# A two-layer hybrid decoder step on one core: reordering the linear attention's masks, convolution taps and norm steps

## The reference

```python
xn = rmsnorm(x); z = xn @ w_in + b_in
o_a = rmsnorm(gla(q, k, v, log_a, state)) * silu(r)      # gated linear attention, chunks of 64
o_b = gelu(u) * spatial(layernorm(gelu(v)))              # gMLP
o_c = silu(layernorm(causal_depthwise_conv31(c_a * sigmoid(c_g))))
o_d = sink_attention(q, k, v)                            # window of 128, learned sinks
x = x + (sum_b sigmoid(xn @ w_gate_b) * (o_b @ w_branch_b)) @ w_out
x = x + swiglu(rmsnorm(x))
```

## Time and profile before

| | |
|---|---|
| median of three runs | 1078.9 us (1078.13 to 1079.26) |
| the profiled execution | 1078.94 us |
| its span, first to last instruction | 1077.1 us |
| outside the span | 1.84 us |
| PE busy in the span | 1070.7 us |
| DVE, ACT, POOL busy | 739.7, 585.9, 454.4 us |

### The profile page before, as it was taken

One profiled execution on the slowest core, in us unless ns is written; L12 is line 12 of the kernel. 1 busy time (PEld: TensorE's weight loads), 2 busy tenths in 40 slices (PEclk: granted clock), 3 DMA queues, 4 the chain that ended last, 5 costly groups with the idle time before them and its releaser, 6 DMA issues.

```text
span 1077.1 us, 20930 instructions
## 1 busy us (share of the span) xinstructions
PE 1070.7 (99%) x8755; PEld 1054.6 (98%) x8755; DVE 739.7 (69%) x1020; ACT 585.9 (54%) x895; POOL 454.4 (42%) x248
## 2 busy tenths in 40 slices
PE   9999999999999999999999999999999999999999
PEld 9999989999999999999999999999999999999998
DVE  6699999565875555555548799894577765555542
ACT  7664654778455444444446656567774564444431
POOL 2777845773742111101177768657737321111000
PEclk9999999999999999999999999999999999999999
DMA  9754553444555765555545555445454655555552
GB/s 294 257 172 162 171 158 103 141 152 155 176 172 185 217 200 185 170 174 162 175 152 158 159 168 181 159 121 155 157 154 140 232 164 170 160 174 161 175 172 83
DMA packets 65053, 182.53 MB, mean 169 GB/s; under 512 B 17056, under 2 KB 21792, under 8 KB 64288
## 3 DMA queue, kind: packets, MB, share of 16 engines
q1 hardware_dynamic: 63952, 177.12, 52.6%
q10 hardware_dynamic: 1008, 4.08, 1.0%
HBM read 174.90 MB, written 7.27 MB: 169 GB/s over the span
## 4 chain that ended last, share of the span: by engine, by line
PE 89%; DVE 10%; ACT 1%; issue 0%; DVEq 0%; ACTq 0%
PE ps L457 29%; PE ps L462 28%; PE ps L458 28%; DVE ps L1380 2%; DVE work L1354 1%; PE ps L780 1%; DVE zg L1454 1%; DVE work L1429 1%; PE ps L657 0%; DVE qz L1507 0%; PE ps L477 0%; DVE hist_p L1340 0%; DVE zg L1446 0%; DVE zg L1447 0%; DVE work L1445 0%
## 5 line engine op out<-in xcount | busy, mean ns | idle before, releaser
L457 PE MATMUL ps<-x_hi,w_hi 128*128 128x288 f32 x1952 | 583.2, 299 | 0.0
L458 PE MATMUL ps<-x_lo,w_hi 128*128 128x288 f32 x1952 | 575.8, 295 | 0.0
L462 PE MATMUL ps<-x_hi,w_lo 128*128 128x288 f32 x1952 | 574.0, 294 | 0.0
L930 ACT ACTIVATE w_hi<-raw 128x1024 fp32r<-128x1024 f32 x314 | 326.1, 1052 | 143.2 <-PE ps L462 130.0
L1779 POOL TENSOR_TENSOR w_lo<-raw,w_hi 128x1024 fp32r<-128x1024 f32 x129 | 335.2, 2612 | 162.3 <-ACT w_hi L930 161.1
L457 PEld LDWEIGHTS ps<-x_hi,w_hi 128*128 128x128 f32 x1952 | 365.8, 187 | 6.4 <-issue 4.7
L462 PEld LDWEIGHTS ps<-x_hi,w_lo 128*128 128x128 f32 x1952 | 367.4, 188 | 0.0
L458 PEld LDWEIGHTS ps<-x_lo,w_hi 128*128 128x128 f32 x1952 | 366.5, 188 | 0.4
L1296 DVE TENSOR_TENSOR w_lo<-raw,w_hi 128x1024 fp32r<-128x1024 f32 x185 | 230.1, 1245 | 119.6 <-ACT w_hi L930 119.6
L1803 POOL TENSOR_TENSOR work<-work,rs 128x288 f32<-128x288 f32 x44 | 35.9, 815 | 238.2 <-ACT work L1257 238.2
L462 PE MATMUL ps<-h_hi,w_lo 128*128 128x288 f32 x352 | 104.4, 296 | 0.0
(11 more groups left out here) (249 smaller groups left out, 1076.7 us busy)
## 6 DMA issues: line engine op xcount, KB each, us to landing
raw<-in_w_up SPq DMA_DIRECT2D x88, 512.0 KB, 4.1
raw<-in_w_z SPq DMA_DIRECT2D x66, 512.0 KB, 3.7
raw<-in_w_gate SPq DMA_DIRECT2D x64, 512.0 KB, 3.6
raw<-in_w_branch SPq DMA_DIRECT2D x32, 512.0 KB, 3.6
raw<-in_w_down SPq DMA_DIRECT2D x32, 512.0 KB, 3.5
raw<-in_w_out SPq DMA_DIRECT2D x16, 512.0 KB, 3.6
raw<-in_w_down SPq DMA_DIRECT2D x16, 384.0 KB, 3.3
kv<-in_state ACTq DMA_DIRECT2D x2, 1024.0 KB, 5.0
```

The source lines that it names most:

```text
L457: pe.matmul(out, wh, rh, start=start, stop=False)
L458: pe.matmul(out, wh, rl, start=False, stop=False)
L462: return pe.matmul(out, w_lo[:, slot, u * UNIT:(u + 1) * UNIT], rh, start=False, stop=stop)
L930: act.activation(w_hi[:, slot, :], raw[:, slot, :], ACT.Copy).then_inc(hi_done, 1)
```

## The change

- In ACT's generator `conv0` moves behind `k_copied`, to place 41.
- In DVE's order for layer 0, the convolution steps ahead of segment 11 (the masks) go from 14 to 4 and those ahead of segment 12 from 3 to 10. In layer 1 those ahead of segment 12 go from 3 to 0. What is not run by then is run later, in segment 17 at the latest.
- Scores are kept with their sign turned: the score step multiplies by `-HD ** -0.5` and subtracts the mask, the reduction is a minimum, and the exponential is taken with `scale=-1.0`. `softmax_in` then has two instructions in place of three.
- The differences for `to_last` are two instructions for both key tiles in place of four.
- `conv1`, `cv_mean`, `cv_sq`, `gla_sums`, `gla_rstd`, `gla_spread`, `r_silu`, `c_silu`, `a_parts` and `smp_update0` go two places later. `gm_mean`, `gates0` and all that follows keep their places.

```diff
-    chunk1=42, chunk2=43, chunk3=44, gla_spread=53, n1_sums=0, n1_rstd=0, n1_sums0=3, n1_rstd0=3, c_gate0=12,
+    chunk1=42, chunk2=43, chunk3=44, gla_spread=55, n1_sums=0, n1_rstd=0, n1_sums0=3, n1_rstd0=3, c_gate0=12,
-    exp0=20, exp1=31, prompt_pv=36, prompt_od=37, smp_scores=27, conv0=40,
-    conv1=48, exp_s=30, probs_s_turned=34, probs_s_copied=35, smp_pv=36, smp_od=37, decay_in=24, decay_y=16, decay_log=17,
+    exp0=20, exp1=31, prompt_pv=36, prompt_od=37, smp_scores=27, conv0=41,
+    conv1=50, exp_s=30, probs_s_turned=34, probs_s_copied=35, smp_pv=36, smp_od=37, decay_in=24, decay_y=16, decay_log=17,
-    gla_o=37, cv_mean=49, cv_sq=50, smp_update0=57, smp_update1=58, gla_sums=52, gla_rstd=52, cv_var=39, r_silu=54,
-    c_silu=56, a_parts=51, gates0=60, gm_mean=60, gm_sq=61, gm_var=63, gv_done=64, gv_turned=65, gv_copied=68,
+    gla_o=37, cv_mean=51, cv_sq=52, smp_update0=59, gla_sums=54, gla_rstd=54, cv_var=39, r_silu=56,
+    c_silu=58, a_parts=53, gates0=60, gm_mean=60, gm_sq=61, gm_var=63, gv_done=64, gv_turned=65, gv_copied=68,
-CONV_RUNS = (8, 1, 0, 0, 0, 2, 0, 0, 0, 3, 6, 14, 3, 2, 3, 4, 4, 5, 2, 4, 9, 10, 8, 9, 10, 7, 3,
-             8, 2, 0, 4, 5, 2, 0, 0, 0, 3, 3, 7, 3, 2, 3, 4, 4, 0, 6, 7, 4, 13, 0, 11, 13, 7, 3)
+CONV_RUNS = (8, 1, 0, 0, 0, 2, 0, 0, 0, 3, 6, 4, 10, 2, 3, 4, 4, 5, 2, 4, 9, 10, 8, 9, 10, 7, 3,
+             8, 2, 0, 4, 5, 2, 0, 0, 0, 3, 3, 7, 0, 2, 3, 4, 4, 0, 6, 7, 4, 13, 0, 11, 13, 7, 3)
...
                 act.wait_ge(E("v_turned"), l1)
-                yield from at("conv0")
-                conv_out(l, 0)
                 yield from at("k_copied")
                 act.wait_ge(E("k_turned"), l1)
+                yield from at("conv0")
+                conv_out(l, 0)
...
-                link(dve.tensor_tensor(small[:, 0, cols], small[:, 0, cols], p("sink", 0, 18)[:, cols], ALU.max), l)
-                dve.tensor_scalar(small[:, 1, cols], small[:, 0, cols], -1.0, None, ALU.mult)
-                dve.tensor_tensor(small[:, 2, cols], p("sink", 0, 18)[:, cols], small[:, 0, cols], ALU.subtract)\
-                    .then_inc(E(event), 1)
+                sink = p("sink", 0, 18)[:, cols]
+                link(dve.scalar_tensor_tensor(out=small[:, 1, cols], in0=sink, scalar=-1.0, in1=small[:, 0, cols],
+                                              op0=ALU.mult, op1=ALU.min), l)
+                dve.tensor_tensor(small[:, 2, cols], sink, small[:, 1, cols], ALU.add).then_inc(E(event), 1)
...
-                for k in range(2):
-                    v, w = to_last[:, k, 0:SEQ].rearrange("p (n i) -> p n i", i=64), decays[:, k, 0:SEQ].rearrange("p (n i) -> p n i", i=64)
-                    dve.tensor_tensor(v, w[:, :, 63:64].to_broadcast([P, NSEG, 64]), w, ALU.subtract)
-                    v, w = to_last[:, k, SEQ:T].rearrange("p (n i) -> p n i", i=DEC_T), decays[:, k, SEQ:T].rearrange("p (n i) -> p n i", i=DEC_T)
-                    ins = dve.tensor_tensor(v, w[:, :, DEC_T - 1:DEC_T].to_broadcast([P, DEC_B, DEC_T]), w, ALU.subtract)
+                v, w = (a[:, :, 0:SEQ].rearrange("p k (n i) -> p k n i", i=64) for a in (to_last, decays))
+                dve.tensor_tensor(v, w[:, :, :, 63:64].to_broadcast([P, 2, NSEG, 64]), w, ALU.subtract)
+                v, w = (a[:, :, SEQ:T].rearrange("p k (n i) -> p k n i", i=DEC_T) for a in (to_last, decays))
+                ins = dve.tensor_tensor(v, w[:, :, :, DEC_T - 1:DEC_T].to_broadcast([P, 2, DEC_B, DEC_T]), w, ALU.subtract)
-                                         scalar=HD ** -0.5, in1=bcast(c("band", P, P), 8), op0=ALU.mult, op1=ALU.add)\
+                                         scalar=-HD ** -0.5, in1=bcast(c("band", P, P), 8), op0=ALU.mult, op1=ALU.subtract)\
-                link(dve.tensor_reduce(small[:, 0, 0:8], prob0, AX.X, ALU.max), l)
+                link(dve.tensor_reduce(small[:, 0, 0:8], prob0, AX.X, ALU.min), l)
...
```

## The result

| | before | after |
|---|---|---|
| median of 7 runs each | 1079.11 us (1078.13 to 1079.26) | 1081.92 us (1081.3 to 1083.03) |
| ratio, 95% interval | | 1.003 [1.0021, 1.0039] |
| profiled execution | 1078.94 us | 1082.99 us |

The change made the kernel slower by 2.8 us, 0.3%. The forecast was 1082.4 us.

What follows compares the result with a forecast made beforehand. PE was taken as the bound, so only its waits and the slow clock behind them count: -4.4 + 0 + 7.9 = +3.5 us on 1078.94 us gives 1082.4 us, range 1079.0 to 1087.5 us.

Steps and rivals of the forecast that it cites:

- What bounds the kernel: PE is busy 1070.7 of 1077.1 us, so the change acts only through PE's waits and the slow clock behind them.
- Part 1: `conv0` behind `k_copied`, masks ahead of taps: layer 0's 2.6 us pause at `chunks` and 1.8 us slow clock go, -4.4 us.
- The state step: First state copy, layer 0 at `chunk1`: 1.1 us late by the rows, but taken as no wait; bounds 0 and 1.1 + 1.8 us.
- Part 2: Lighter softmax input and `to_last`: DVE gains 0 to about 3 us a layer, none of it PE's; worth 0.
- Part 3: Norms and state update two tiles later, `gm_mean` staying: 2.6 us wait there per layer plus 1.35 us slow clock, +7.9 us.
- X: Start of L745, PE's state update `smp_update0`, from which times up to `gm_mean` are counted.
- The price of the clock: Slow clock behind each new pause at `gm_mean`: bounds 0 and 1.8 us, three quarters taken, 1.35 us.
- Pause without slow clock: Rival: both waits at `gm_mean` come but PE's clock stays, 1079.7 us; chance 0.2, with one short fall included.
- Port held: Rival: POOL's block falls on DVE's difference L1317 as before, lengthening the waits at `gm_mean`, 1087.5 us; chance 0.1.
- Pause moved to `chunk1`: Rival: the pause at `chunks` only moves to `chunk1`, up to 2.9 of 4.4 us come back, 1085.3 us; chance 0.1.
- Faster, as `gm_mean` hardly waits: Rival: DVE has the sum ready within about a tile; without any wait 1074.5 us; chance 0.08.

Runs made afterwards that it cites:

- norms_one_later: Changed kernel with norm steps and state update one place later than before instead of two, and `gates0` at 59: 1074.62 us, ratio 0.9958.
- conv0_behind: Kernel before with one edit, `conv0` behind `k_copied` at 41 in ACT's order: 1077.8 us, ratio 0.9991.
- norms_back: Changed kernel with norm steps and state update, `conv1` and `gla_spread` back at their old places: 1077.39 us, ratio 0.9985.
- old_softmax: Changed kernel with the old score sign, three instructions in `softmax_in` and four for the differences: 1081.4 us.
- pause_filled: Changed kernel with 18 matmuls whose result nothing reads put ahead of the wait at `gm_mean`: 1080.26 us, ratio 1.0013.
- norms_one_gates60: Changed kernel with norm steps and state update one place later than before instead of two, `gates0` left at 60: 1077.67 us, ratio 0.9989.
- norms_later_alone: Kernel before with only the norm steps and state update moved two places later; `conv0`, taps and softmax as they were: 1086.41 us, ratio 1.0069.

## Why the prediction was right, step by step

**What bounds the kernel.** Right. The places where PE waited, and the clock behind them, account for the difference that matters most: norms_one_later has no wait at a mixer step, and the span of the changed kernel's profiled execution is 1081.2 - 1072.9 = 8.3 us longer; two pauses of 2.5 us and two falls of the clock at 1.6 us (both below) make 8.2. Between the medians it is 1081.92 - 1074.62 = 7.3 us.

**Part 1, -4.4 us.** Right in place and size, as a term of this sum. Between the kernel before and norms_one_later lie 1078.92 - 1074.62 = 4.3 us, and PE took up `chunk1` at 170.68 us before and at 166.56 after. The masks were named as the next cause, and conv0_behind shows them. The state step was named too, but that is less sure: in conv0_behind it was in time in layer 0, with PE held 1.5 us by the masks ahead of it, and late in layer 1, where the prediction saw nothing at stake. Nor is 4.4 us what parts 1 and 2 are worth alone. norms_back gained 1.5 us (1078.93 to 1077.39). Without its pause PE comes to `cv_mean` of layer 0 at 192.44 us in place of 196.23, and DVE's sum ends at 193.72 in place of 195.38, so what had been in time is late. Part 3 takes that wait away again; the prediction has no term for either, and they don't show in the total. In the changed kernel the state copy ended at 165.80 us, against 165.5 forecast, with L1532 at 0.69 us, against an estimate of 0.7.

**Part 2, nothing.** Right (old_softmax). At the place shown, the hold of 2.3 us went over to the next instruction.

**Part 3, +7.9 us.** The mechanism was right, and the size about right: 7.3 us from norms_one_later to the changed kernel, 7.5 us for part 3 on the kernel before. On parts 1 and 2 alone it is 4.5 us (1077.39 to 1081.92), since there it also removes the waits at `cv_mean`. The pause itself was forecast as 2.6 us in each layer, from X + 4.4 to X + 7.0, and was 2.5 us in both, X + 4.4 to X + 6.9. The waits are listed as 2.31 and 2.32 us because the list counts from the modelled end of the last matmul. pause_filled puts 2.37 us of matmuls in the gap, and `gm_mean` then follows with no wait listed.

**The price of the clock, 1.35 us a pause.** This was the term taken with the least ground. The changed kernel's seven runs show what it averages over: three with a mean granted clock of 0.997 took 1082.67 to 1083.03 us, four with 0.998 took 1081.3 to 1081.92. The profiled one, with 0.997, has the fall behind both pauses, as the stretches above show. In the profile of old_softmax, with 0.998, one pause has it and the other not:

```profile
233.80:238.00 4.20, 4.20 (x33) 1.00 0.40 136
...
768.80:773.00 4.20, 4.20 (x23) 0.61 0.48 141
```

So a fall costs about 1.6 us (1082.99 - 1081.41, the medians of the two groups), and not each pause of 2.3 us brings one. The traces give the same price. From the update of layer 0 (L745) to that of layer 1 it is 535.34 us in the changed kernel's profile, with the fall of layer 0 in it, and 533.75 us in that of old_softmax, without. A run thus pays 1.6 or 3.2 us, and the forecast's 2.7 us for both pauses lies between. That four of seven runs had the cheaper case was not foreseen, so the forecast's distance of 0.5 us from the median is in part luck. That is also why the changed kernel's times spread over 1.7 us and those of norms_one_later over 0.3.

**The rivals.** Pause without slow clock: not seen for both pauses in any run of the changed kernel; by its mean clock each run had one fall at least, and four of the seven only one. Port held: not in the changed kernel, but it is what norms_one_gates60 shows. Pause moved to `chunk1`: not here, since DVE was 0.8 us early; conv0_behind shows such a wait, but in layer 1. Faster, as `gm_mean` hardly waits: it took two tiles between the update and the mean, and `gates0` out of the way.

**What stays open.** The kernel before has 44 further runs. In 28 of them the clock was 0.998, in 16 it was 1.000, and the medians are 1079.05 and 1078.30 us: 0.75 us apart, not the 1.8 us that the 16 matmuls of `chunks` lost. The profile of norms_later_alone shows a reason: without the fall PE comes to `chunk1` ahead of the state copy and waits there, which leaves 0.8 us. It is one execution, and of a kernel that differs behind that place. The prediction's full 1.8 us came back in the changed kernel because the state copy came earlier as well. Two of the 16 runs took 1079.13 and 1079.15 us, as long as those with the fall; why is open, and so is what decides whether a pause of this length brings a fall.

## What to carry to other kernels

When a group of steps is moved in a stream that is ordered by place, look at the step that stays: the distance to it is what changes, and the chain that has to fit in that distance can be added up from the trace before. A pause of the matmul engine is to be priced with the slow clock behind it, which here added 1.6 us to 2.5 when it came, and 0.8 us where the next step would have been late anyway. One pause of 2.6 us cost more than two of 1.5 and 1.1 (1078.92 against 1077.8 us). An engine that loses a pause comes earlier to its next wait, so the price of a part depends on which other parts are there: part 3 cost 7.5 us on the kernel before and 4.5 us on parts 1 and 2. An instruction that is held up by another engine's block passes its wait on when it is removed, so what counts is when the block starts, and a step of a third engine can decide that.

## What the runs showed of the hardware

Two things had not been expected. The fall of the clock doesn't come with each pause of about the same length. The pause of 2.6 us in the kernel before brought one in 28 of 44 runs, by the mean clock, and the changed kernel's two pauses of 2.3 us (as listed) brought one or two in every run. The profile of norms_later_alone has a pause of 2.53 us with a clock of 1.00 behind it. No run of the kernels whose longest pause behind the start was 1.3 to 1.5 us (norms_back, norms_one_gates60, conv0_behind, 33 runs) showed a mean clock under 1.000.

And the lower level can set in when PE is back at work. In the changed kernel's first pause PE started again at 233.78 us; its matmuls came 0.13 us apart until 234.50 and 0.24 us apart from then on, so that the pause itself was still at 1.00 and the stretch behind it at 0.59. In norms_later_alone's pause at the same place, PE started again at 237.50 us and its matmuls were 0.24 us apart from 237.88 on, from the second one.
